# Turned attention weights copied ahead of the high parts, and the heads of a pair handled one by one

## What is computed

```python
sh1, sc1, gt1, sh2, sc2, gt2 = modulation(cond, mod_w, mod_b)      # silu(cond) @ mod_w + mod_b
h = rms_norm(x, norm_g[0]) * (1 + sc1) + sh1
z = h @ w_in                                                       # ab_split
conv_out = gate_b * short_conv(gate_c * xin, conv_w)
# latent_attention, blocks of 128 queries, own band of three blocks and 256 cached keys
s = q @ k.T * scale                                                # band: |kpos - qpos| <= 128
p = softmax(concatenate([s_loc, s_ctx, sink]))[..., :-1]
o = p @ v
out = concatenate([conv_out, attn]) @ w_out
```

## Time and profile before

| | |
|---|---|
| median of the runs | 3106.9 us (3103.04 to 3114.9, 3 runs) |
| the profiled execution | 3106.81 us, span 3105.0 us |
| PE busy | 2880.5 us, 93% of the span |
| DVE busy | 1592.2 us, 51% |
| ACT busy | 1359.0 us, 44% |
| granted PE clock, mean | 0.97 |

### The profile page before, as it was taken

The page is one execution under the profiler, slowest core; times in us unless marked ns, Lnnn a source line. Parts: engine busy times, 40 slices in busy tenths (PEclk is TensorE's granted clock), DMA queues, the critical chain, the costliest instruction groups (busy, mean ns, idle before and its releaser), DMA issues. The chain is left out here.

```text
span 3105.0 us, 39476 instructions
## 1 busy us (share of the span) xinstructions
PE 2880.5 (93%) x14994; PEld 2493.3 (80%) x14994; DVE 1592.2 (51%) x2337; ACT 1359.0 (44%) x2157; POOL 159.4 (5%) x260
## 2 busy tenths in 40 slices
PE   5898878889999999999999998777899999999998
PEld 3666766667999999999989776776789999999997
DVE  6455645555454554554431355787454545445444
ACT  6344444454443443433331466554344434334333
POOL 0000000000000000000000003880000000000000
PEclk8999998999999999999999999888999999999999
DMA  6442122153444434444422442002534444444443
GB/s 238 142 151 79 58 82 68 55 155 103 123 125 125 147 122 123 148 124 127 123 70 62 136 129 88 7 1 91 181 109 122 123 128 142 128 128 143 128 128 109
DMA packets 309733, 355.12 MB, mean 114 GB/s; under 512 B 20086, under 2 KB 242748, under 8 KB 308572
## 3 DMA queue, kind: packets, MB, share of 16 engines
q1 hardware_dynamic: 300560, 331.52, 34.4%
q10 hardware_dynamic: 7020, 13.87, 1.3%
q0 software_dynamic: 2016, 7.86, 0.7%
HBM read 337.88 MB, written 15.34 MB: 114 GB/s over the span
## 5 line engine op out<-in xcount | busy, mean ns | idle before, releaser
L1260 DVE TENSOR_TENSOR p_lo<-p_raw,p_hi 128x1024 fp32r<-128x1024 f32 x507 | 619.6, 1223 | 743.7 <-ACT p_hi L724 743.2
L724 ACT ACTIVATE p_hi<-p_raw 128x1024 fp32r<-128x1024 f32 x507 | 533.1, 1052 | 569.2 <-DMA p_raw<-mlp_w 423.9
L2025 PE MATMUL ps<-hm_hi,p_hi 128*128 128x384 f32 x1536 | 515.7, 336 | 4.8 <-DVE hm_lo L1280 4.0
L2025 PE MATMUL ps<-hm_hi,p_lo 128*128 128x384 f32 x1536 | 515.8, 336 | 0.0
L2025 PE MATMUL ps<-hm_lo,p_hi 128*128 128x384 f32 x1536 | 514.4, 335 | 0.0
L1964 PE MATMUL ps<-p_hi,hid_hi 128*128 128x512 f32 x1152 | 363.5, 396 | 5.1 <-DVE p_lo L1260 5.1
L1964 PE MATMUL ps<-p_lo,hid_hi 128*128 128x512 f32 x1152 | 358.8, 393 | 0.0
L1964 PE MATMUL ps<-p_hi,hid_lo 128*128 128x512 f32 x1152 | 357.4, 392 | 0.0
L940 ACT ACTIVATE relu<-ps 128x384 f32<-128x384 f32 x192 | 94.5, 492 | 525.5 <-PE ps L2025 525.5
L1498 DVE TENSOR_TENSOR sqr<-relu 128x384 f32<-128x384 f32 x192 | 107.1, 558 | 377.8 <-ACT relu L940 377.8
L2025 PEld LDWEIGHTS ps<-hm_hi,p_hi 128*128 128x128 f32 x1536 | 288.4, 188 | 14.1 <-DVE hm_lo L1280 4.5
(11 more groups left out here) (238 smaller groups left out, 4093.6 us busy)
## 6 DMA issues: line engine op xcount, KB each, us to landing
p_raw<-mlp_w SPq DMA_DIRECT2D x384, 512.0 KB, 4.0
mod_p<-mod_w SPq DMA_DIRECT2D x80, 512.0 KB, 4.0
p_raw<-gla_w_in SPq DMA_DIRECT2D x56, 512.0 KB, 3.6
p_raw<-gla_w_out SPq DMA_DIRECT2D x24, 512.0 KB, 3.3
mod_w<-mod_w SPq DMA_DIRECT2D x8, 1024.0 KB, 13.0
p_raw<-ab_w_in SPq DMA_DIRECT2D x14, 512.0 KB, 5.4
p_raw<-ab_w_out SPq DMA_DIRECT2D x12, 512.0 KB, 3.6
p_raw<-ab_w_out SPq DMA_DIRECT2D x24, 256.0 KB, 3.9
```

What stands on the lines that cost most here:

```text
L724: nc.scalar.activation(p_hi[s][:, :, 0:width], p_raw[s][:, :, 0:width], ACT.Copy).then_inc(pan_hi, 1)
L1260: V.tensor_tensor(p_lo[s][:, :, 0:width], p_raw[s][:, :, 0:width], p_hi[s][:, :, 0:width].bitcast(F32), ALU.subtract).then_inc(pan_lo, 1)
L2025: mm = M.matmul(ps[:, b, 0:GN], w[s][:, c, :], x[:, c, :], start=(c == 0 and x is hi and w is p_hi), stop=(c == DC - 1 and w is p_lo))
```

## The change

Five things differ. ACT's `turned_weights` stands right behind `unit_take`, and the high parts of the next unit and the panel's high part behind it. DVE's `normalise` stands right behind `maxima`, and the low parts behind it. The semaphores `s_exp`, `s_norm` and `pt_ready` count heads and not pairs, so that the sink's exponential, the add and the reciprocal, the scaling, the five transposes and the copy out of PSUM are each done head by head. The high part of panel p+1 is made in the first unit of panel p (n == 0) and its low part in the second (n == 1), where both were made in the third unit of panel p-1. And the release of a panel's slot does not ride on the transposes of a pair that is 128 columns wide.

```diff
@@ -811,18 +811,17 @@
                 out, n = weights(p)[0], pair_width(p)
                 for u in range(2):
                     act.wait_ge(s_max, 2 * p + u + 1)
-                    nc.scalar.activation(wide(out[u])[:, 0:n], s_bank(u)[:, 0:n],
-                                         ACT.Exp, bias=x[:, 1, u:u + 1], accum_out=x[:, 2, u:u + 1])
-                for u in range(2):
+                    nc.scalar.activation(wide(out[u])[:, 0:n], s_bank(u)[:, 0:n], ACT.Exp, bias=x[:, 1, u:u + 1],
+                                         accum_out=x[:, 2, u:u + 1])
                     head = p % 4 + 4 * u
-                    last = nc.scalar.activation(x[:, 3, u:u + 1], sink[:, head:head + 1], ACT.Exp, bias=x[:, 1, u:u + 1])
-                last.then_inc(s_exp, 1)
+                    nc.scalar.activation(x[:, 3, u:u + 1], sink[:, head:head + 1], ACT.Exp,
+                                         bias=x[:, 1, u:u + 1]).then_inc(s_exp, 1)
 
             def turned_weights(p):
 
-                act.wait_ge(pt_ready, p + 1)
                 n = pair_width(p)
                 for u in range(2):
+                    act.wait_ge(pt_ready, 2 * p + u + 1)
                     last = nc.scalar.activation(wide(weights(p)[1][u])[:, 0:n], s_bank(u)[:, 0:n], ACT.Copy)
                 last.then_inc(pt_a, 1)
 
@@ -839,13 +838,15 @@
                     late_rows(q)
                 if pair is not None:
                     exps(pair)
-                for k in mods_after(u + 1):
-                    late_hi(k)
                 if pair:
                     output_take(pair - 1)
                 unit_take(u)
-                if n == 2 and p + 2 < IN_PANELS:
-                    panel_split_hi((p + 2) % 3, pieces=2 if 2 <= p + 2 < 6 else 1)
+                if pair is not None:
+                    turned_weights(pair)
+                for k in mods_after(u + 1):
+                    late_hi(k)
+                if n == 0 and 0 < p < IN_PANELS - 1:
+                    panel_split_hi((p + 1) % 3, pieces=2 if 2 <= p + 1 < 6 else 1)
                 if 6 <= u < 9:
                     act.wait_ge(v_turned, u - 5)
                     nc.scalar.activation(v_n[:, GT * (u - 6):GT * (u - 5), :],
@@ -857,8 +858,6 @@
                     act.wait_ge(kc_read, 1)
                     act.dma_start(io["new_cache_k"][0, 0].rearrange("s h d -> s (h d)"), k_out[:]).then_inc(cache_out, 16)
                     act.dma_start(io["new_cache_v"][0, 0].rearrange("s h d -> s (h d)"), v_n[:, 0, :]).then_inc(cache_out, 16)
-                if pair is not None:
-                    turned_weights(pair)
             for q in rows_after(UNITS):
                 late_rows(q)
             output_take(PAIRS - 1)
@@ -1392,13 +1391,12 @@
             def normalise(p):
 
                 x, n = smx[:, p % 2], pair_width(p)
-                dve.wait_ge(s_exp, p + 1)
-                own(V.tensor_tensor(x[:, 2], x[:, 2], x[:, 3], ALU.add))
-                own(V.reciprocal(x[:, 0], x[:, 2]))
                 for u in range(2):
+                    dve.wait_ge(s_exp, 2 * p + u + 1)
+                    own(V.tensor_tensor(x[:, 2, u:u + 1], x[:, 2, u:u + 1], x[:, 3, u:u + 1], ALU.add))
+                    own(V.reciprocal(x[:, 0, u:u + 1], x[:, 2, u:u + 1]))
                     pr = wide(weights(p)[0][u])[:, 0:n]
-                    last = V.tensor_scalar(pr, pr, x[:, 0, u:u + 1], None, ALU.mult)
-                last.then_inc(s_norm, 1)
+                    V.tensor_scalar(pr, pr, x[:, 0, u:u + 1], None, ALU.mult).then_inc(s_norm, 1)
 
             for u in range(UNITS):
                 p, n = divmod(u, GROUPS)
@@ -1407,16 +1405,16 @@
                     dve.wait_ge(att_in, 64)
                 if pair is not None:
                     maxima(pair)
+                if pair is not None:
+                    normalise(pair)
                 for k in mods_after(u):
                     late_lo(k)
-                if pair is not None:
-                    normalise(pair)
                 if rope_after(u) is not None:
                     rope(rope_after(u))
                 if u > CONV_UNIT:
                     conv(u - 1)
-                if n == 2 and p + 2 < IN_PANELS:
-                    split_lo((p + 2) % 3)
+                if n == 1 and 0 < p < IN_PANELS - 1:
+                    split_lo((p + 1) % 3)
                 for q in rows_after(u):
                     late_add(q)
             conv(UNITS - 1)
@@ -1856,13 +1854,13 @@
 
             def turn_weights(p):
 
-                pe.wait_ge(s_norm, p + 1)
                 for u in range(2):
+                    pe.wait_ge(s_norm, 2 * p + u + 1)
                     for i in range(pair_width(p) // P):
                         last = turn(s_bank(u)[:, i * P:(i + 1) * P], weights(p)[0][u][:, i, :])
-                        if i == 0 and u == 0:
+                        if i == 0 and u == 0 and pair_width(p) > P:
                             used_before(last)
-                last.then_inc(pt_ready, 1)
+                    last.then_inc(pt_ready, 1)
 
             def output(p):
```

## The result

The changed kernel takes 3006.85 us (median, 3003.57 to 3012.46), the one before 3104.97 (3102.01 to 3114.9): a ratio of 0.968, 95% interval 0.9653 to 0.9708, faster by 98 us. The forecast of 3023 had the direction and the mechanism, but the gain is 14 us larger, the kernel before came out 2 us lower than the 3106.8 that it was counted from, and the time lies 1 us under the low end of the range, 3008.

What follows compares the result with a forecast made beforehand. PE idling behind ACT's and DVE's queue order, and its lowered clock, were taken as the bound. Waits of 60 us plus 26 of clock gave 86, the control 82; 84 was taken: 3106.8 - 84 = 3023 us, range 3008 to 3062.

Steps and rivals of the forecast that it cites:

- What bounds it, and that the waits go: Units from 204 to 650 us: PE idles 71.2 us, 65.9 of it waiting for turned weights, scaled weights and output takes.
- the sum: Sum by waits over the pairs: 65.9 - 3 - 1.5 - 1 = 60 us of waits, and 26 of clock: 86 us.
- Turned weights ahead of the high parts: ACT's queue: copying turned weights when the unit is taken cuts PE's 53.4 us of waits to some 3.
- What that pushes back: ACT's high parts and next exponentials, queued behind the copies, still fit: 0.2 to 1 us spare at the tightest place.
- Panels "cost nothing": Panels' high and low parts made later on ACT and DVE: no cost; without cover, at most 12 panels times 1.2 us.
- Heads one by one, low parts behind: DVE's chain from maxima to scalings: 5.3 us where it was 5.85; PE's 8.3 us wait for scalings becomes about 1.5.
- The clock: PE's clock, slowed behind long waits, recovers over the pairs' stretch: 26 us taken, between ends of 0 and 31.
- The rival, that the transposes lower it: PE's clock falls behind the transposes and four-row products ending every pair: 26 us stay, 3049; chance 0.09.
- The control sum by kinds: Pairs counted by kind at full clock: 24 take 242 us for 308.6, 67 saved; 15 from the others: 82 together.
- Ahead of pair 0, plus or minus 1: Before unit 18, the panels' move puts an ACT copy ahead of one v copy and behind another: plus or minus 1 us.
- DVE does not become the bound: Rival on DVE: low parts or maxima 0.9 us late in each pair, 32 us stay, 3055; chance 0.15.
- The exponentials do not starve: Rival on ACT: high parts awaiting loads delay the next exponentials; 3179 at a 14 us landing; chance 0.04 for slower.

## Why the prediction was right or wrong

- *What bounds it, and that the waits go*: right. PE's idle time in the pairs fell by 61.8 us; the sum had 60 and was 1.8 short.
- *Turned weights ahead of the high parts*: right in the mechanism. 53.4 us became 1.8, where 3 was expected, 0.4 to 0.5 us for each unit without a part. The second copy ends 0.80 us behind the transposes in pair 19 (380.58 to 381.38); how the half microsecond is made up no run shows, and a copy that waits for a transpose starts 0.04 us behind its end where the rows show it (379.86 and 379.90 with the panels put back). But it was priced as if on its own. Alone it gives 35 us, and taken out it costs 90.
- *What that pushes back*: right for the changed kernel. ACT is done with the panel's high part at 373.22 and idles 2.14 us until the maxima let the first exponential start.
- *Panels "cost nothing"*: wrong as a price. The move is worth 17 to 20 us. In the third unit the panel's high part would stand behind two high parts, and DVE's low part of it, with the maxima behind, would wait for it. I had looked for who waits behind ACT's exponentials only, and not at DVE's own queue. The sum, being for all parts together, was not touched.
- *Heads one by one, low parts behind*: right, and mis-sized. The term took the 8.3 us of recorded waits for scaled weights down to 1.5. The working had the chain at 5.85 us against 5.9 of cover, a tie, and booked no gain where no idle row stood. But the wait was there in nearly every pair, under the tail of the unit's last product: PE's busy time fell by 29.4 us in the pairs, of which the clock explains 26.1, half of the 52.1 us of busy time at the low level. The other 3.3 are such tails, and the sum had nothing for them.
- *The clock*: right, in size too. All lowered stretches in the pairs went, and I took 26 of 31 where they cost 26.1. The rival, that the transposes lower it, fell with the changed kernel's 1.00.
- *The control sum by kinds*: one of the two steps that failed. It took 9.55 us for a one-part pair, from a busy time of 9.43 in a pair that had waits; the measured one is 9.12. The other kinds are too long as well (10.4 for 10.9, 10.1 for 10.5, 9.2 for 9.4). Busy time read beside a wait holds the tails of products that overlap once the wait is gone. The sum gave 82 and should have warned that 86 was too little; instead it pulled the forecast down to 84. With the measured kinds it is 11 x 9.12 + 5 x 10.1 + 6 x 10.4 + 2 x 9.15 = 232, 77 saved and 92 in all.
- *Ahead of pair 0, plus or minus 1*: the other step that failed. It is 4.3 us, and by the wrong part. It comes with the ACT order, which I had costed within the pairs alone, as if the rest of the program held none of the edited code, though the order is written for all 54 units. The gain stands in units 6 to 9, 38.3 us before and 34.3 after; which wait of the knot went first there these runs do not separate.
- *The rest*: 2.9 us shorter in the changed profile. In the fourteen profiles it is 2480 to 2491 with almost no code of it changed (only the last unit's), and 2482 in the changed kernel's second; I take it for scatter, which no run shows for certain.
- *What the 14 us are made of*: 4.3 ahead of pair 0, 3.4 of busy time beyond the 26 of clock, 2.0 by which the control sum pulled the forecast down, 1.8 of idle time, and the 2.9. The range was missed by 1 us only, so that without any one of these the time would have been inside: the mechanism held, and what failed are the terms at nothing.
- *The rivals*: DVE does not become the bound (PE waits 2.4 us for low parts, mostly in the first pairs). The exponentials do not starve. The rival that I missed is the one that the ACT order alone shows: a panel's low part that holds DVE's maxima back, and low parts that still stand ahead of the scalings, 35 us of waits. Even that kernel is faster than the one before.
- *The low end*: 3005 was all idle time and all lowered clock, called out of reach, and so 3008. Hidden tails and the units ahead of pair 0 were not in that bound.

## What to carry to other kernels

When a queue holds work that another engine waits for behind work that itself waits for that engine, put the waited-for work first; and then list what the move pushes in front of the next urgent instruction, since alone it may only move the knot. Parts of such a change are not to be priced one at a time: singly they gave some 42 us here, together 98. And a pair's cost at full speed is to be read from start to start in a stretch without waits; busy time beside a wait counts tails that overlap as soon as the wait is gone.

## What the runs showed of the hardware

- PE's recorded idle understates what a wait costs: in the one-part pair with the heads together, 0.46 us of idle stood for 0.9 us of length.
- Waits of up to 2.0 us ahead of 24 pairs left the clock at 0.98, with the low level behind the four waits of 1.7 and 2.0 us only; waits of up to 4.9 us ahead of 32 pairs brought it to 0.84 and cost 64 us of busy time beside 115 of idle time. With 36 stretches of transposes and no waits to speak of it was 1.00.
- The four parts of the change taken out one at a time cost 90, 24, 20 and 18 us, 152 in all (by the ratios 87, 23, 16 and 16) where the whole is worth 98: with one wait left in, part of what the others give is lost again.
